# Nine projection pairs per layer by Strassen's scheme, with their weight sums on GpSimd

## What is computed

```
h = rms_norm(x, P['norm_mix'][l])
z = jnp.einsum('btd,dn->btn', h, P['w_in'][l])
a_q, a_k, a_v, b_q, b_k, b_v, b_g, b_lr, c_qkv, c_z, c_b, c_a, gates = jnp.split(z, split_points(), axis=-1)
```

## Time and profile before

| what | value |
|---|---|
| device time, median of 3 runs | 1810.05 us |
| lowest and highest of the 3 | 1804.7 and 1813.07 us |
| span of the profiled execution | 1802.1 us |
| PE busy | 1748.8 us, 97% |
| DVE, ACT, POOL busy | 743.5 us, 364.3 us, 154.3 us |
| DMA, mean | 313 GB/s |

### The profile page before, as it was taken

The page is one execution under the profiler, slowest core; times in us unless marked ns, Lnnn a source line. Parts: engine busy times, 40 slices in busy tenths (PEclk is TensorE's granted clock), DMA queues, the critical chain, the costliest instruction groups (busy, mean ns, idle before and its releaser), DMA issues.

```text
span 1802.1 us, 30183 instructions
## 1 busy us (share of the span) xinstructions
PE 1748.8 (97%) x12542; PEld 1282.9 (71%) x12542; DVE 743.5 (41%) x1548; ACT 364.3 (20%) x760; POOL 154.3 (9%) x259
## 2 busy tenths in 40 slices
PE   9999999999999999999999998999989999999997
PEld 7889888787768999978898887877663343333423
DVE  3444542434535765534544414355342332233222
ACT  2241333433101000012313333331011110100001
POOL 3000000403200111000100002032000000000000
PEclk9999999999999999999999999999999999999999
DMA  9833599999999997899535899899958999999994
GB/s 296 285 120 100 187 324 316 359 310 367 388 347 392 365 321 286 288 348 371 194 107 207 308 325 346 312 350 384 333 211 327 393 377 414 402 398 394 371 415 177
DMA packets 265853, 563.96 MB, mean 313 GB/s; under 512 B 14654, under 2 KB 163362, under 8 KB 265441
## 3 DMA queue, kind: packets, MB, share of 16 engines
q1 hardware_dynamic: 246384, 500.15, 76.8%
q0 software_dynamic: 18544, 58.58, 9.2%
q10 hardware_dynamic: 784, 3.26, 0.5%
HBM read 547.75 MB, written 196.63 MB: 413 GB/s over the span
## 4 chain that ended last, share of the span: by engine, by line
PE 85%; SPq 7%; DMA 4%; DVE 2%; issue 1%; ACT 1%; DVEq 0%; POOL 0%; ACTq 0%; POOLq 0%
PE PS L940 34%; PE PS L1598 8%; PE PS L1374 8%; SPq L811 7%; PE PS L1350 5%; PE PS L1382 4%; PE PS L859 3%; PE PS L986 3%; PE PS L1576 3%; PE PS L1364 2%; PE PS L979 2%; PE PS L1636 2%; PE PS L1321 1%; PE PS L1537 1%; DMA mem<-bias_tables 1%
## 5 line engine op out<-in xcount | busy, mean ns | idle before, releaser
L940 PE MATMUL PS<-h,mem 128*128 128x264 f32 x2816 | 654.3, 389 | 0.0
L940 PEld LDWEIGHTS PS<-h,mem 128*128 128x128 f32 x2816 | 527.8, 191 | 106.7 <-issue 21.3
L1806 ACT COPY z<-PS 128x264 f32<-128x264 f32 (+5 forms) x293 | 119.5, 430 | 737.6 <-PE PS L940 527.6
L1598 PE MATMUL PS<-mem,z 128*32 128x512 f32 (+1 forms) x1536 | 146.1, 523 | 3.8 <-DMA mem<-in_moe_w_up 3.8
L2893 DVE COPY small<-mem 128x1024 f32 x56 | 38.8, 693 | 175.6 <-PE PS L1576 117.8
L1598 PEld LDWEIGHTS PS<-mem,z 128*32 128x32 f32 x1536 | 47.4, 110 | 77.8 <-issue 61.2
L1576 PE MATMUL PS<-small,z 128*32 128x256 f32 (+2 forms) x624 | 86.9, 396 | 1.3 <-DVE z L2893 1.3
L1350 PE MATMUL PS<-z,mem 128*128 128x264 f32 x384 | 87.3, 388 | 0.0
L1576 PE MATMUL PS<-z 128*32 128x256 f32 (+2 forms) x624 | 87.0, 396 | 0.0
L1350 PEld LDWEIGHTS PS<-z,mem 128*128 128x128 f32 x384 | 72.3, 190 | 13.8 <-issue 1.7
L1374 PE MATMUL PS<-z,mem 128*128 128x132 f32 x624 | 78.3, 278 | 0.0
(11 more groups left out here) (377 smaller groups left out, 2028.2 us busy)
## 6 DMA issues: line engine op xcount, KB each, us to landing
out_win_s<-in_cache_win_kv SPq DMA_DIRECT2D x128, 1023.5 KB, 11.9
mem<-in_w_in SPq DMA_DIRECT2D x88, 1024.0 KB, 7.6
mem<-in_moe_w_gate SPq DMA_DIRECT2D x80, 512.0 KB, 9.7
mem<-in_moe_w_up SPq DMA_DIRECT2D x80, 512.0 KB, 8.9
mem<-in_moe_w_down SPq DMA_DIRECT2D x64, 512.0 KB, 13.6
out_win_s<-in_cache_win_kv SPq DMA_DIRECT2D x32, 1022.0 KB, 13.1
z<-in_moe_w_down SPq DMA_DIRECT2D x48, 512.0 KB, 13.1
z<-in_moe_w_up SPq DMA_DIRECT2D x32, 512.0 KB, 10.6
```

The costliest lines, as they stand in the source:

```text
L940: last = mm(bank(l, "p", j)[:, 0:T], w[:, k, P * (j % 2):P * (j % 2) + P], h[:, k, :], start=(k == 0), stop=(k == KT - 1))
L1598: last = mm(m_bank("c", "gu", g, b, w, r)[BLK * j:BLK * j + BLK, 0:n], hs[:, k, P * r + BLK * j:P * r + BLK * j + BLK], v3(slot_ap(set_slo ...
L1806: return nc.scalar.copy(out, in_)
```

## The change

The pairs 23 to 31 of each layer (tiles 46 to 63) are computed in four steps in place of two: `fold_x`, `fold_y`, `fold_x2`, `fold_y2`. Together they are seven products of four matmuls with 132 columns. `fold_x` and `fold_x2` use bank 0, `fold_y` and `fold_y2` bank 1.

- **Weight sums.** POOL makes four sums of 128 x 512 per chunk (`fold_w`), a pair ahead of PE. Two sets of buffers alternate; a set is free when the pair two back is finished. `fold_x` waits for the third of the sums after its first product.
- **Input sums.** DVE makes four sums of `h` (`fold_h`, 128 x 528 each). They lie where `x` lay. So SP stores `x` to memory (`x_kept`, 1.08 MB) before the load of chunk 5, and loads it back behind the load of chunk 36, when pair 31 is done. `fold_h` stands in the list right behind tile 3 and waits until the store has landed.
- **Results.** DVE combines the products from PSUM: two reduces, a small sum and a sum of 264 per pair. ACT copies one quarter in place of two tiles.
- **Other.** POOL's `kv_tok` also waits for pair 29. Two small GLA buffers are moved, and the counters that the feed-forward of layer 0 waits on start higher.

```diff
+FOLD = tuple(range(23, 32))
...
+    def tile(j):
+        q = j // 2
+        if q not in FOLD:
+            return [("proj", j)]
+        return [("fold_x2", q), ("fold_y2", q)] if j % 2 else [("fold_x", q), ("fold_y", q)]
...
+    s.insert(s.index(("proj", 3)) + 1, ("fold_h",))
+    for q in FOLD:
+        before = ("fold_x", q - 1) if q - 1 in FOLD else ("proj", 2 * q - 2)
+        s.insert(s.index(before) + 1, ("fold_w", q))
     return s
...
+                    if n == RING:
+                        sp.wait_ge(sems["h_ready"], V("h_ready", l, KT - 1))
+                        sp.dma_start(x_kept[l], x_flat).then_inc(x_in, 16)
                     load(CH0[l] + n, source(l, n))
+                    if n == FOLD[-1] + RING:
+                        wait_full(sp, l, "fold_y2", FOLD[-1])
+                        sp.wait_ge(x_in, 64 + 32 * l)
+                        sp.dma_start(x_flat, x_kept[l]).then_inc(x_in, 16)
...
+            def fold_x(l, q):
+                wait_chunk(pe, CH0[l] + q)
+                open_bank(pe, l, "fold_x", q)
+                x_ = bank(l, "fold_x", q)
+                four(x_[:, 0:HALF], fold_quarters(l, q)[0], h[:, 0:4, 0:HALF], True)
+                pe.wait_ge(hd_ready, h_sum(l, 3))
+                pe.wait_ge(fw_even, even_sum(l, q, 1))
+                four(x_[:, HALF:T], fold_sums(q)[1], fold_t[:, 1]).then_inc(full(l, "fold_x", q), 1)
...
+            def fold_x2(l, q):
+                open_bank(pe, l, "fold_x2", q)
+                four(bank(l, "fold_x2", q)[:, 0:HALF], fold_quarters(l, q)[1], h[:, 4:8, 0:HALF]).then_inc(
+                    full(l, "fold_x2", q), 1)
...
+            def fold_h(l):
+                dve.wait_ge(x_in, 64 + 32 * l)
+                h11, h12, h21, h22 = h[:, 0:4, 0:HALF], h[:, 0:4, HALF:T], h[:, 4:8, 0:HALF], h[:, 4:8, HALF:T]
+                tt(fold_t[:, 0], h12, h11, SUB)
+                tt(fold_t[:, 2], h22, h12, SUB).then_inc(hd_ready, 1)
...
+            def fold_x(l, q):
+                if q != FOLD[0]:
+                    wait_read(dve, l, "fold_y2", FOLD[FOLD.index(q) - 1])
+                wait_full(dve, l, "fold_x", q)
+                nc.vector.tensor_reduce(fold_ve[:, 0, :], bank(l, "fold_x", q)[:, 0:T].rearrange("p (w t) -> p t w", w=2),
+                                        AX.X, ADD).then_inc(free(l, "fold_x", q), 1)
...
+            def fold_w(l, q):
+                wait_chunk(pool, CH0[l] + q)
+                if fold_before(q) is not None:
+                    wait_full(pool, l, "fold_y2", fold_before(q))
...
+                a11, a12, a21, a22 = fold_quarters(l, q)
+                s1, s2, s4 = fold_sums(q)
+                tt(s1, a21, a22, ALU.add)
+                tt(a21, a11, a21, ALU.subtract).then_inc(fw_odd, 1)
+                pool.wait_ge(fw_odd, odd_sum(l, q))
+                tt(s2, a22, a21, ALU.subtract).then_inc(fw_even, 1)
+                pool.wait_ge(fw_even, even_sum(l, q, 1))
+                tt(s4, a12, s2, ALU.subtract).then_inc(fw_even, 1)
```

More of the change, by code:

```diff
@@ L52 @@
 S_TAB, S_KEY, S_SELF, S_TOT = 0, NG * 512, NG * 512 + NG * P, NG * 512 + NG * P + NS
+HALF = T // 2
+UNSETTLED = ("proj", "fold_x", "fold_y", "fold_x2", "fold_y2", "fold_w")
+FOLD = tuple(range(23, 32))
 WARM = 12
@@ L81, in schedule @@
     proj = iter(range(Z_N))
+    def tile(j):
[3 more added lines that the diff above has]
+        return [("fold_x2", q), ("fold_y2", q)] if j % 2 else [("fold_x", q), ("fold_y", q)]
     def p(n=1):
-        return [("proj", next(proj)) for _ in range(n)]
+        return [step for _ in range(n) for step in tile(next(proj))]
     s += p() + [("small_turn",)] + p(2) + [("conv_v", 0)] + p() + [("gate_c",)] + p() + [("conv_v", 1)]
@@ L92, in around @@
         j = next(proj)
-        return [step, ("proj_half", j), (step[0] + "2", *step[1:]), ("proj", j)]
+        first, rest = tile(j) if j // 2 in FOLD else (("proj_half", j), ("proj", j))
+        return [step, first, (step[0] + "2", *step[1:]), rest]
     for i in range(TT):
@@ L596, in wait_z @@
         def wait_z(eng, l, lo, hi):
-            for j in range(max(lo, hi - 2), hi):
+            for j in [j for j in range(lo, hi) if j // 2 not in FOLD][-2:]:
                 wait_read(eng, l, "p", j)
+            for q in [q for q in FOLD if lo <= 2 * q + 1 and 2 * q < hi][-1:]:
+                wait_read(eng, l, "fold_x2", q)
+                wait_read(eng, l, "fold_y2", q)
         CH0 = [0, CH_MIX + CH_FFG + CH_FFD]
@@ L612, in build @@
             for q in range(CH_PROJ):
-                place(n0 + q, q % RING, (l, "p", 2 * q + 1))
+                place(n0 + q, q % RING, (l, "fold_y2", q) if q in FOLD else (l, "p", 2 * q + 1))
             for q in range(CH_WB):
@@ L1766, in experts @@
                         turn_y(d)
-            run = dict(params=params, tables=tables, small=small_step, small_turn=small_turn, proj=proj, proj_half=proj_half, conv_s=conv_s, conv_t=conv_t, gate_c=gate_c,
-                       norm_sum=norm_sum, gdn_dec=gdn_dec, gdn_a=gdn_a, gdn_a2=gdn_a2,
+            run = dict(params=params, tables=tables, small=small_step, small_turn=small_turn, proj=proj, proj_half=proj_half, fold_x=fold_x, fold_y=fold_y, fold_x2=fold_x2,
+                       fold_y2=fold_y2, conv_s=conv_s, conv_t=conv_t, gate_c=gate_c, norm_sum=norm_sum, gdn_dec=gdn_dec, gdn_a=gdn_a, gdn_a2=gdn_a2,
                        gdn_lv=gdn_lv, gdn_lv2=gdn_lv2, gdn_st=gdn_st, gdn_st2=gdn_st2,
@@ L1843, in proj, with fold_x2 @@
                 copy(z[:, j, :], bank(l, "p", j)[:, 0:T]).then_inc(free(l, "p", j), 1)
+            def fold_x2(l, q):
+                wait_full(act, l, "fold_x2", q)
+                copy(fold_out(q)[:, 0:HALF], bank(l, "fold_x2", q)[:, 0:HALF]).then_inc(free(l, "fold_x2", q), 1)
             def small_turn(l):
@@ L2052, in _ @@
             act.dma_start(con[:, 2 * P:K_TOT], a["const_main"][:, 2 * P:K_TOT]).then_inc(con_rest, 16)
-            run = dict(tables=tables, small_turn=small_turn, proj=proj, conv_a=conv_a, cz=cz, gate_c=gate_c, norm_sq=norm_sq,
+            run = dict(tables=tables, small_turn=small_turn, proj=proj, fold_x2=fold_x2, conv_a=conv_a, cz=cz, gate_c=gate_c, norm_sq=norm_sq,
                        norm_sum=norm_sum, gdn_dec=gdn_dec, gdn_a=gdn_a, gdn_lv=gdn_lv, gdn_st=gdn_st,
@@ L2060, in _ @@
                     if step[0] in run:
-                        if step[0] != "proj":
+                        if step[0] not in UNSETTLED:
                             settle()
```

115 lines of the change are left out of this document (95 added, 20 removed).

## The result

The changed kernel takes 1809.95 us, the median of 20 runs (1805.48 to 1814.05). Twenty runs of the kernel before, taken with them, have a median of 1804.76 us. The ratio is 1.0025, with a 95% interval of 1.0014 to 1.0035: the change costs 4.5 us, a quarter of a per cent, where the forecast had a gain of 1.9. The three runs of before that the prediction started from had a median of 1810.05, so the 7.9 us that it added to the span were 2.7 in the longer series; the forecast's 1808.2 came near the measured time, which lies inside its range of 1797 to 1816, by that accident: from 1804.76 the same sum would have given 1802.9. Ratios and intervals are taken over fast runs alone (one of 5556.6 us and one of 2598.5, in the experiments, are left out) and need not be the ratio of the two medians. The span of the profiled execution went from 1802.1 to 1807.8.

The account below looks back on a forecast made before the run. PE was taken to set the pace, with room on POOL and DVE and none on DMA. The terms -14.8 + 1.6 + 5.4 + 5.9 = -1.9 us gave a median of 1808.2 us, range 1797 to 1816.

Parts of the forecast that it names:

- pair 31 and the tables: Last pair before the first scores: shorter, but tables come no sooner, so PE waits 0.82 longer per layer, +1.6 us.
- POOL and DVE at once: Six places per layer where POOL's sums lengthen DVE instructions that PE soon needs: +5.4 us, range 0 to +15.
- PE's products: Folded `proj` pairs on PE take 6.30 us in place of 7.12: 14.8 saved for 18 pairs.
- The tables: Bias tables' landing at the first scores, sharing queues with returning `x`: 0 taken, 0 to 2.1 us per layer kept.
- POOL's sums: POOL's sums of 512 columns take an estimated 1.26 us each, finish in time for PE, and cost 0.
- Rival B: POOL becomes the bound at PE's second product of each pair; at 2.7 us a sum, +16, so 1826; chance 0.09.
- DVE's combining: DVE's 1.6 us of combining per pair frees bank 0 for `fold_x2` with 0.1 to spare; cost 0 undisturbed.
- the twelve places of the prediction: Both layers' `norm_sum` 3, 4, 6, 7, 8 and `gx_m` with `norm_sum` 5, each delayed 0.52 us by POOL.
- the 7.6 that the prediction worked out for the rule: POOL and DVE excluding each other whole: twelve waits of half a sum, 7.6 us, making the sum 2.2 later.
- Parking `x`: Layer 1's late store delays `fold_h`; PE waits 4.2 us at tile 6, plus 1.7 for the clock: +5.9.
- Rival A: Store lands before 802 and POOL and DVE miss each other, so no waits: -13.2 us, 1796.9; chance 0.22.

Follow-up runs that it names:

- 8-column sums: Changed kernel with each of POOL's four sums per pair cut to 8 columns in place of 512; 2725.83 us, a total that can't be used.
- Parking alone: Kernel before, nine pairs computed plainly and no POOL sums, with `x` stored, overwritten and reloaded; 1804.72 us, ratio 1.0001 to before.
- the one with POOL's waits: Changed kernel with whole sums, POOL waiting ahead of five of the nine to keep clear of DVE's norms; 1796.90 us, ratio 0.9966 to before.
- the best version: Changed kernel with POOL's waits, reduces of pairs 28 to 31 ahead of the norms on DVE, `fold_h` before the first norm; 1794.52 us, ratio 0.9952.
- The sums alone: Kernel before, plain pairs and `x` not parked, with POOL's sums added; 1816.31 us, ratio 1.0066; repeated 1817.73, ratio 1.0071.

## Why the prediction was wrong, by its own steps

It had the direction wrong. Its terms against what was measured, in the profiled executions, all in us:

| term | predicted | measured | from |
|---|---|---|---|
| products, 16 pairs ahead of `norm_sum` 9 | -13.1 | -12.5 | stages with 8-column sums |
| pair 31 and the tables | 0 | +2.2 | table of marks |
| POOL and DVE at once | +5.4 | +10.2 | the two stages, changed kernel less 8-column sums |
| store of `x`, tile 6 of layer 1 | +5.9 | +4.9 | table of marks |
| the rest | 0 | +0.8 | table of marks |
| sum | -1.9 | +5.6 | |

- *PE's products*: right. The chain gives 6.41 to 6.45 for the 56 records, where 6.30 was taken. The 0.1 stands at `fold_x2`, whose first eight records take 1.17 where the others take 1.06; the prediction charged nothing there.
- *The tables*: that PE would gain nothing there held. That their landing costs 0 did not, in this profile: 9.87 and 11.36 against 8.37 and 10.49. It is within the bound of 0 to 2.1 a layer. No run ties it to `x`: with `x` parked and plain pairs the same way was shorter than before, and the changed kernel run again had 13.34 in layer 0 where the first had 14.14. I leave it as scatter of these transfers.
- *POOL's sums*: right, 1.27 in place of 1.26, and POOL was never the bound. Rival B does not come.
- *DVE's combining*: right. PE's waits at `fold_x2` are small until pair 31 (1.1), but for one of 0.9 in layer 1, behind the long row of norm 7.
- *POOL and DVE at once*: **this is the step that failed**: +5.4 was taken, and 10.2 measured. Three things in it were off, and the first two nearly cancel.
  - The price of a meeting was taken from the one row that showed one, +0.52, where POOL's instruction took 0.74. POOL's take 1.27 here, and DVE's rows are longer by anything from nothing (norm 8, 1.32) to 1.03, at norm 7 of layer 1, where they start together. Over the twelve places of the prediction they are longer by 4.4 us in all, where 12 times 0.52 is 6.2.
  - The meeting with the two instructions of `norm_sum` 2, while POOL makes the sums of pair 24, was not among the places: 1.2 us in layer 0, 0.95 in layer 1. I had counted only norms that stand before a reduce, and this one stands before `gs_c`, where the PE of before waits for nothing. With it the part at full clock, 10.2 less 5.1, came out near the 5.4, which is luck. PE's idle time accounts for 3.2 of these 5.1 (2.7 and 3.2 us in the two stages, 1.4 in each with 8-column sums); where the rest lies the rows don't show.
  - The clock: I charged PE's wait of 4.2 at tile 6 with a half clock and these short waits with none. Three half clocks, 1.7 each, are the other 5.1, and most of what lay between the forecast and the result.
- The Trainium skill's rule (page "SBUF — State Buffer", section "Who interferes with whom"), by which the two engines' instructions exclude each other whole, is what the rows at 230.9 to 235.9 show: 2.29 and 2.21 where 1.27 and 1.26 stand undisturbed. The prediction called the row of before milder than the rule, because 0.52 was paid where 0.66 of POOL's instruction was left. That was a misreading: it is short by 0.14, as are the rows here (0.13 to 0.15). The row agreed with the rule; what was wrong was to carry its 0.52 to POOL instructions of another length. With the 7.6 that the prediction worked out for the rule, the forecast would have been +0.3, on the right side, and still without the clock.
- *Parking `x`*: right in each link. The size was 1.0 too large, since PE itself came 1.7 later and waited 3.0 in place of 4.2. It also depends on when the store lands: in the other profiles with `fold_h` in this place and folded pairs PE waited 1.3 to 1.9, and no half clock came. What it costs on average is open. Parking alone measures 1.0001 (0.9982 to 1.0020), which has room for 3.6 us but not for the 5.9 that I charged; but moving `fold_h` away took 0.4% off the changed kernel, and nothing off the one with POOL's waits.
- Rival A, that the waits don't come, is what the best version makes true by its order: its ratio of 0.9952 is 8.7 us below before, where the rival's sum was 13.2.

The runs together settle that the meeting of sums and norms is what undoes most of the gain: taken away by order, with the work unchanged, it gives back the time and most of the clock, in the changed kernel (1.0025 to 0.9966) and in the plain one with the sums added (1.0071 to 1.0002). What stays open is which short wait is followed by a half clock and which is not, and how much the place of `fold_h` adds in the changed kernel.

## What to carry to other kernels

Work moved to an idle engine is free only if its operands' path is free as well: here GpSimd was busy for 57 of 100 us with them, and they still cost 10 us because they stood beside VectorE instructions with two inputs in SBUF that TensorE was about to need. Look in the trace of before for those instructions, and place the new work between them by a wait; that cost nothing here and was worth 0.6%. And charge each wait that a change adds to TensorE, short ones too, with the chance of a half clock behind it, which can cost more than the wait.

## What the runs showed of the hardware that was not expected

- A very short instruction of POOL waits for DVE's whole one too. In the run with 8-column sums one that takes 0.20 elsewhere took 1.22, beside DVE's second instruction of `norm_sum` 2, which ends at 233.03. POOL first, then DVE, of that run:

```profile
231.71 0.20 POOL L3214 TENSOR_TENSOR mem<-mem 128x8 f32<-128x8 f32 x1
231.87 1.22 POOL L3215 TENSOR_TENSOR mem<-mem 128x8 f32<-128x8 f32 x1
```

```profile
231.72 1.31 DVE L2425 TENSOR_TENSOR z<-z,mem 128x1056 f32<-128x1056 f32 x1
```

- It strikes DVE's small instructions too. The 132-column sum of the two reduces takes 0.30, and in the changed kernel at worst 1.45. Line L2366, least, median and greatest ns:

```profile
L2366 DVE TENSOR_TENSOR z<-fold_ve x18: 296/298/1446, 244.6 to 1090.7; 128x132 f32<-128x132 f32 x18
```

- A wait of PE as short as 0.5 us was followed by 3.4 us at 1.2 GHz in some executions and not in others of the same code. The sums alone had the same two waits in layer 0, 0.5 and 2.1 us, in both of its profiled executions. In the one the clock was 0.56 behind the first (above); in the other it stayed whole:

```profile
236.90:240.40 3.50, 3.50 (x16) 2.65 (x15) 2.70 (x5) 0.00 (x0) 1.13 (x2) 1.00 1.06 421
```

  The spans were 1810.4 and 1803.0. In layer 1 the execution of 1803.0 has a half clock too, behind its wait of 2.1. So one profile can hide what the runs pay on average, and the mean clock of all runs (0.9867 to 0.9869 for this code, 0.991 before) is the better witness.
